# Results kept by channel: attention, gates and Fourier outputs of the first layer of a two-layer network

## The chip, the cores and the metric

One core of a Trainium2 chip. The metric is the time of one execution on the device, in microseconds (us); lower is better. The kernel before takes 3724.84 us, the median of three runs (3721.65 to 3726.13).

## The reference

A network of two layers over T = 2304 tokens (256 of context, 2048 latent) of width 1024. The change concerns the first layer alone:

```
h = layer_norm(x) * (1 + scale) + shift
q, ga, k, v, u, gb = split(h @ w_in)          # 768, 768, 256, 256, 256, 256
q, k = rope(rms_norm(q)), rope(rms_norm(k))   # 12 query heads of 64, 4 key heads
a = softmax(q k^T / 8) v                      # latent tokens see all 2304 keys, context tokens its own 256
f = real(fft2(rms_norm(u))) @ w_fmix
y = concat(a * silu(ga), f * silu(gb)) @ w_out
x = layer_norm(alpha * x + g * y) * gain + bias
```

The second layer (a bidirectional mLSTM) takes the result as its input. Everything is fp32, or products split into a high and a low part.

## The kernel before, in words

The program is written out for each engine: each has its own instruction order, and semaphores tie them. Tokens are handled in 18 tiles of 128. The stages run one after another: modulation, projections of layer 0 (names `pj_`, with the query heads `hq_` between them), key heads with the context's attention (`hd_`, `ca_`), attention of the latent tokens (`al_`), Fourier mix (`fo_`), the output of the mixer (`mo_`); then layer 1 (`pa_`, `pb_`, `ml_`, `mo_`).

**Projections** (`projections`). Steps k run over chunks c of 512 columns (five) and in each over the 18 tiles. A step multiplies a tile of `h`, split in `h_hi` and `h_lo` (stationary), with `whi` and `wlo` (512 columns moving): 8 slices of 128 channels, three products each (L245 to L247), into one of three PSUM banks. ScalarE (chunk 0 and, with SiLU, the gate chunks c = 3 and 4, L762) or VectorE copies the bank to `pj_stage` in the same step, and SyncE stores it to `s_proj`, token by token. Between these, every third step from k = 21 on, runs a tile of query heads: SyncE reloads the tile's queries and rope rows, ScalarE squares (L299), VectorE sums and turns, TensorE transposes (L370), ScalarE and VectorE take high and low part from PSUM (L306, L362), SyncE stores both to `s_q`.

**Context attention** (`ContextAttention`), twelve heads, its steps spread over the tiles of `heads`. The result stands token by token, with the sum of the weights in column 65; VectorE divides two columns (L1812) and multiplies 128x128 (L1814); POOL stores each head to `s_attn`.

**Attention** (`attention`). 48 blocks, each one query head with 512 tokens. TensorE computes all scores twice: first (`high_scores`, L2346) query by query in 20 products into three scratch banks `slots` (shown as `al_sx`), of which VectorE takes the maxima (L2269), and at the end of them the bias row `negm` (L2275). SyncE carries that row with four small DMAs (L2158) into the query operand `al_qb` of the block. The second time (`scores`, L2358/L2359), keys on the partitions, in nine pairs j of key tiles; ScalarE takes the exponential (L2209). The products with the values (L2368) go to the bank `acc`, even key tiles in partitions 0 to 63, odd ones in 64 to 127. POOL and VectorE add the nine pairs of exponentials (`al_asum`). The order in a body is the same on each engine: the body of block n holds the high scores of block n+1, the scores of n, and at its head the last values of n-1, which ScalarE copies to `al_ot` (L2216). Behind the scores of j = 7 TensorE runs `folded` for block n-1:

```
for i in range(nq):
    mm(fo[:, at:at + HD], ot[:, p % 2, cols], fold[:, 0:HD], start=True, stop=True)
    y = mm(fo[:, at + HD:at + HD + 1], asum[:, p % 2, cols], ones[:], start=True, stop=True)
```

It adds the two halves, turns the result to tokens and sums `asum` over partitions. `fo` is the third scratch bank. At j = 8 VectorE divides (L2290) and multiplies (L2294), and SyncE stores (L2164).

**Fourier** (`fourier`). 18 results of 128 tokens, token by token, copied by VectorE and stored to `s_four`; the loads of the out weights (`ow_wst`, two buffers) stand between the stores on SyncE, and ScalarE and POOL split them (L2452, L2456).

**Mixer's output** (`mixer_out`). Per tile: SyncE loads `attn`, `four` and the gate (`mo_in`), VectorE multiplies (`gated`, L2845), TensorE transposes 8 times (L2890), ScalarE takes the high part (L2759) and VectorE the low one (L2849), TensorE multiplies with the out weights (48 products of 512 columns), and VectorE and POOL add, norm and scale. `gated` runs two tiles ahead.

## Time and profile before

| | |
|---|---|
| runs (three) | 3724.84 us median, 3721.65 to 3726.13 |
| the profiled execution | 3726.69 us |
| its span on the core | 3724.9 us |
| TensorE | busy 3439.9 us (92%) |
| VectorE | 2280.6 us (61%) |
| ScalarE, GpSimd | 1336.0 us (36%), 1821.1 us (49%) |
| DMA | 480.18 MB, mean 129 GB/s |
| mean granted clock of TensorE | 0.959 of full speed |

PE is TensorE's products, PEld its weight loads, DVE VectorE, ACT ScalarE, POOL GpSimd, SP SyncE (SPq: its DMA issues). A row of a group says: line, engine, operation, what is written from what, shape, count, busy time and mean of one. "Idle before" is the time in which the engine did nothing ahead of it, with the instruction that ended it. The records of products overlap, since they are pipelined: the distance of two starts is what one costs.

### The profile page before, as it was taken

To read this page: it belongs to the slowest core of one execution; us is meant where nothing else is said; L and a number is where in the kernel's file an instruction comes from. 1 tells how busy PE (TensorE), PEld (TensorE's weight loads), DVE (VectorE), ACT (ScalarE), POOL (GpSimd) and SP (SyncE) were. 2 spreads that over 40 slices of the span, in tenths; PEclk is the share of its full clock that TensorE was granted. 3 is DMA by queue.
4 is the path that set the end of the run, shared out by engine and by line. 5 is a ranking of instruction groups with operands and counts; after the bars stand their busy time and mean duration, and the time that the engine had idled before them with its cause. 6 is when DMAs were issued, how large, how long until landed. Compare 5 with 4: busy or idle time off the path is not lost. (4 is left out here: it accounts for less than half of the span.)

```text
span 3724.9 us, 51223 instructions
## 1 busy us (share of the span) xinstructions
PE 3439.9 (92%) x16884; PEld 2590.2 (70%) x16884; DVE 2280.6 (61%) x3492; ACT 1336.0 (36%) x2240; POOL 1821.1 (49%) x1260
## 2 busy tenths in 40 slices
PE   6999997799999999999959979989999998999798
PEld 4787884456666666666548869878778786887587
DVE  4666642766666666666536664366575645777566
ACT  2432333434444444444420023333443422664300
POOL 1133323657777777777723333423586612444354
PEclk8999997799999999999979989999999999999899
DMA  5334535511111111111054445655545446677553
GB/s 189 99 107 132 142 105 177 191 27 35 34 35 34 34 35 36 36 38 35 17 198 166 166 166 171 203 186 158 180 129 172 140 151 197 215 220 243 201 210 146
DMA packets 357715, 480.18 MB, mean 129 GB/s; under 512 B 83308, under 2 KB 209276, under 8 KB 357392
## 3 DMA queue, kind: packets, MB, share of 16 engines
q1 hardware_dynamic: 296640, 360.01, 30.9%
q10 hardware_dynamic: 54256, 97.73, 8.8%
q0 software_dynamic: 6624, 19.94, 1.4%
q8 instruction: 109, 1.79, 0.2%
q14 instruction: 86, 0.70, 0.1%
HBM read 339.75 MB, written 137.72 MB: 128 GB/s over the span
## 5 line engine op out<-in xcount | busy, mean ns | idle before, releaser
L2269 DVE TENSOR_REDUCE al_mx<-al_sx 128x1 f32<-128x512 f32 (+1 forms) x960 | 562.6, 632 | 267.2 <-PE al_sx L2346 253.8
L2209 ACT ACTIVATE al_e<-al_st 128x1024 f32<-128x1024 f32 x432 | 443.1, 1027 | 579.4 <-PE al_st L2359 570.6
L2239 POOL TENSOR_TENSOR al_acc_p<-al_acc_p,al_e 128x1024 f32<-128x1024 f32 x192 | 457.4, 2382 | 19.8
L245 PE MATMUL pb_acc<-p_whi,pb_r_hi 128*128 128x512 f32 x952 | 378.5, 398 | 41.5 <-DVE pb_r_lo L1616 31.6
L2368 PE MATMUL al_acc<-al_e,vres 128*64 128x512 f32 x1728 | 402.5, 601 | 0.0
L247 PE MATMUL pb_acc<-p_whi,pb_r_lo 128*128 128x512 f32 x952 | 375.5, 394 | 0.0
L246 PE MATMUL pb_acc<-p_wlo,pb_r_hi 128*128 128x512 f32 x952 | 375.2, 394 | 0.0
L1616 DVE TENSOR_TENSOR pb_r_lo<-pb_stg,pb_r_hi 128x512 fp32r<-128x512 f32 x238 | 247.8, 1044 | 168.7 <-ACT pb_r_hi L1514 164.4
L2358 PE MATMUL al_st<-al_qa,kres 128*128 128x512 f32 x864 | 344.7, 399 | 3.7 <-DMA al_qb<-al_negm 3.2
L2359 PE MATMUL al_st<-al_qb,kres 128*128 128x512 f32 x864 | 340.3, 394 | 0.0
L2346 PE MATMUL al_sx<-kres,al_qx 128*128 128x512 f32 (+1 forms) x960 | 298.3, 393 | 13.4 <-DMA al_qx<-s_q 11.1
L2235 POOL TENSOR_TENSOR al_acc_p<-al_e 128x1024 f32<-128x1024 f32 x48 | 160.4, 3341 | 305.5 <-ACT al_e L2209 305.5
L245 PE MATMUL pj_acc<-pj_whi,pj_h_hi 128*128 128x512 f32 x720 | 286.8, 398 | 0.0
L2346 PEld LDWEIGHTS al_sx<-kres,al_qx 128*128 128x128 f32 x960 | 172.0, 191 | 162.3 <-issue 125.8
L246 PE MATMUL pj_acc<-pj_wlo,pj_h_hi 128*128 128x512 f32 x720 | 282.9, 393 | 0.0
L247 PE MATMUL pj_acc<-pj_whi,pj_h_lo 128*128 128x512 f32 x720 | 282.7, 393 | 0.0
L855 DVE TENSOR_TENSOR pj_h_lo<-pj_hall,pj_h_hi 128x1024 fp32r<-128x1024 f32 x90 | 135.1, 1502 | 210.3 <-ACT pj_h_hi L723 210.3
L2368 PEld LDWEIGHTS al_acc<-al_e,vres 128*64 128x64 f32 x1728 | 111.2, 136 | 211.2 <-issue 194.9
L1514 ACT ACTIVATE pb_r_hi<-pb_stg 128x512 fp32r<-128x512 f32 x238 | 149.4, 629 | 270.8 <-PE pb_acc L247 248.6
L245 PEld LDWEIGHTS pb_acc<-p_whi,pb_r_hi 128*128 128x128 f32 x952 | 181.3, 190 | 86.8 <-DVE pb_r_lo L1616 38.1
L245 PE MATMUL mo_acc<-ow_whi,mo_y_hi 128*128 128x512 f32 x544 | 215.6, 396 | 0.0
L246 PE MATMUL mo_acc<-ow_wlo,mo_y_hi 128*128 128x512 f32 x544 | 212.7, 391 | 0.0
(318 smaller groups left out, 7261.4 us busy)
## 6 DMA issues: line engine op xcount, KB each, us to landing
pb_stg<-s_hsum ACTq DMA_DIRECT2D x238, 256.0 KB, 2.8
s_proj<-pj_stage SPq DMA_DIRECT2D x90, 256.0 KB, 2.1
s_proj<-pb_out SPq DMA_DIRECT2D x72, 256.0 KB, 2.9
p_wst<-in_w1s ACTq DMA_DIRECT2D x18, 1024.0 KB, 6.5
ml_k<-s_proj SPq DMA_DIRECT2D x36, 512.0 KB, 4.3
ml_v<-s_proj SPq DMA_DIRECT2D x36, 512.0 KB, 8.7
mo_in<-s_proj SPq DMA_DIRECT2D x34, 512.0 KB, 5.7
hm_w<-in_ada_w SPq DMA_DIRECT2D x16, 1024.0 KB, 9.7
```

Of the source, the lines that this page charges most:

```text
L245: nc.tensor.matmul(out, s_hi, m_hi, start=start, stop=False)
L246: nc.tensor.matmul(out, s_hi, m_lo, start=False, stop=False)
L247: return nc.tensor.matmul(out, s_lo, m_hi, start=False, stop=stop)
L1616: V.tensor_tensor(r_lo[:, g % RING], stg[:, g % NSTG], r_hi[:, g % RING].bitcast(F32), ALU.subtract).then_inc(lo_done, 1)
L2209: nc.scalar.activation(e[:, pair(p, j), :, :], st[(NP * p + j) % 2][:, :, 0:W], ACT.Exp).then_inc(e_done, 1)
L2235: nc.gpsimd.tensor_tensor(acc_p[:], e[:, pair(p, 2)], e[:, pair(p, 5)], ALU.add).then_inc(add_p, 1)
L2239: nc.gpsimd.tensor_tensor(acc_p[:], acc_p[:], e[:, pair(p, j)], ALU.add).then_inc(add_p, 1)
L2269: V.tensor_reduce(mx[:, x:x + 1], slots[x % NSX][:, 0:spans[x % NS][1]], AX.X, ALU.max).then_inc(sx_max, 1)
L2346: mm(slots[x % NSX][:, 0:width], qx[:, p, i * P:(i + 1) * P], kres[:, g, lo:lo + width], start=True, stop=True).then_inc(sx_mm, 1)
L2358: mm(dst[:, t, 0:W], kres[:, g, keys], qa[:, p, :], start=True, stop=False)
L2359: y = mm(dst[:, t, 0:W], kres[:, NKV + g, keys], qb[:, p, :], start=False, stop=True)
L2368: y = mm(acc[t * HD:(t + 1) * HD, 0:W], vres[:, 2 * j + t, g, :], e[:, pair(p, j), t, :], start=(j == 0), stop=(j == NP - 1))
```

## The change

Five parts, all in layer 0.

1. *Projections.* In the gate chunks the weights become stationary and four tiles of tokens (512 columns) move, so gates leave by channel, into a new tensor `s_gt` (1024 x 2304). The products of four tiles are accumulated in four banks at once: the first two steps of such a quad run channels 0 to 511 for four column groups of the weights, the other two the rest. Five banks rotate in place of three, a step's eviction stands two steps later, `h_hi`/`h_lo` have four buffers. The last two tiles of a chunk form a pair (256 columns moving). The query heads' rows have two buffers in place of three, and share memory with the rotated products.
2. *Context attention* leaves by channel as well; one division (128x256) and two products (64x256) for two heads, a step later, and one store for two heads.
3. *Attention.* The fold is gone. VectorE adds the two halves itself (`joined`, L2376), behind the second maximum of a body, from PSUM and from ScalarE's copy of one half; the values of a block wait for it. Two blocks stand one above the other in `un` (ScalarE moves the even one: `keep_even`). TensorE sums `asum` of both blocks by two products of 512 columns (`denominators`, L2472) at j = 7 of every second body; VectorE divides 128x512 (L2381) at j = 8 there, and multiplies 128x512 (L2390) at j = 8 of the next body. Two DMAs store two blocks by channel.
4. *Fourier* writes by channel, and stays in SBUF (`four`); its stores are gone.
5. *Mixer's output.* No transposes. `attn` and the gates are loaded by channel (rows of 128 tokens, 512 bytes each), `gated` works in place and stands ahead of `norm`; high and low part read SBUF. The loads wait for the low part of the tile two ahead.

VectorE, attention, one body (names: `al_negm` the bias row, `al_rden` the divisors, `al_o` the result). Before, one body:

```order
L2269 TENSOR_REDUCE al_mx<-al_sx 128x1 x8
L2283 TENSOR_TENSOR al_acc_d<-al_e 128x1024
L2269 TENSOR_REDUCE al_mx<-al_sx 128x1 x8
L2286 TENSOR_TENSOR al_acc_d<-al_acc_d,al_e 128x1024
L2269 TENSOR_REDUCE al_mx<-al_sx 128x1 x4
L2275 TENSOR_REDUCE al_negm<-al_mx 128x4
L2290 RECIPROCAL al_rden<-al_sx 128x4
L2294 TENSOR_TENSOR al_o<-al_sx,al_rden 128x256
```

Now, from the end of an even body on:

```order
L2357 TENSOR_REDUCE al_negm<-al_mx 128x4
L2381 RECIPROCAL al_rden<-al_sx 128x512
L2351 TENSOR_REDUCE al_mx<-al_sx 128x1 x2
L2376 TENSOR_TENSOR al_even<-al_acc,al_ot 64x512
L2351 TENSOR_REDUCE al_mx<-al_sx 128x1 x6
L2365 TENSOR_TENSOR al_acc_d<-al_e 128x1024
L2351 TENSOR_REDUCE al_mx<-al_sx 128x1 x8
L2368 TENSOR_TENSOR al_acc_d<-al_acc_d,al_e 128x1024
L2351 TENSOR_REDUCE al_mx<-al_sx 128x1 x4
L2357 TENSOR_REDUCE al_negm<-al_mx 128x4
L2390 TENSOR_TENSOR al_o<-al_un,al_rden 128x512
```

The division stands once in two bodies, between the bias row and the next maxima, and the sum of the halves behind the second maximum of each body; the multiplication closes the other body.

TensorE, attention, scores of j = 7 and 8 (`al_st`) and the values behind them (`al_acc`). Before, in each body:

```order
L2359 MATMUL al_st<-al_qb,kres 128x512
L2380 MATMUL al_sx<-al_fold,al_ot 128x64
L2381 MATMUL al_sx<-al_ones,al_asum 128x1
L2380 MATMUL al_sx<-al_fold,al_ot 128x64
L2381 MATMUL al_sx<-al_ones,al_asum 128x1
L2380 MATMUL al_sx<-al_fold,al_ot 128x64
L2381 MATMUL al_sx<-al_ones,al_asum 128x1
L2380 MATMUL al_sx<-al_fold,al_ot 128x64
L2381 MATMUL al_sx<-al_ones,al_asum 128x1
L2358 MATMUL al_st<-al_qa,kres 128x512
```

Now, in every second body:

```order
L2453 MATMUL al_st<-al_qb,kres 128x512
L2468 ISA
L2470 REGISTER_ALU
L2472 MATMUL al_sx<-al_asum,al_ones 64x512 x2
L2448 REGISTER_ALU
L2452 MATMUL al_st<-al_qa,kres 128x512
```

Eight products (two instructions each in the trace) are gone from each body; two stand in every second one.

VectorE, mixer's output, one tile. Before:

```order
L2826 BN_AGGR mo_mv<-mo_stats 128x2
L2849 TENSOR_TENSOR mo_y_lo<-mo_tp,mo_y_hi 128x1024
L2831 TENSOR_SCALAR mo_r<-mo_r,mo_mv,mo_rstd 128x1024
L2835 TENSOR_TENSOR mo_fin<-mo_r,mo_gain 128x1024
L2845 TENSOR_TENSOR mo_y<-mo_in 128x1024
```

Now:

```order
L2911 BN_AGGR mo_mv<-mo_stats 128x2
L2942 TENSOR_TENSOR mo_y_lo<-mo_in,mo_y_hi 128x1024
L2927 TENSOR_TENSOR mo_in<-mo_in 128x768
L2929 TENSOR_TENSOR mo_in<-four,mo_in 128x256
L2916 TENSOR_SCALAR mo_r<-mo_r,mo_mv,mo_rstd 128x1024
L2920 TENSOR_TENSOR mo_fin<-mo_r,mo_gain 128x1024
```

The gating product is two, and ahead of the norm.

The core of the diff, in the order of the parts:

```diff
-    K, RING, NST, NACC, PIECES, NX = len(steps), 3 if L0 else 4, 3, 3, 2, 3
+    K, RING, NST, NACC, PIECES, NX = len(steps), 4, 3, 3, 2, 3
     by_act = [c == 0 or (L0 and c >= GATED) for c, _ in steps]
     KP = KD // PIECES
     mod = keep["mod"]
-    turned_q = [not L0 and C1_Q <= c * CH < C1_Q + D for c, _ in steps]
-    pair_of = [k - (t - CT) % 2 if turned_q[k] else k for k, (_, t) in enumerate(steps)]
-    last_use = [pair_of[k] + 1 if turned_q[k] else k for k in range(K)]
-    ahead = [min(K - 1, k + (1 if c == 0 else 2)) for k, (c, _) in enumerate(steps)]
+    turned_q = [c >= GATED if L0 else C1_Q <= c * CH < C1_Q + D for c, _ in steps]
+    base = [k - t % 4 if turned_q[k] else k for k, (_, t) in enumerate(steps)]
+    tiles = [min(4, NT - steps[base[k]][1]) if turned_q[k] else 1 for k in range(K)]
+    last_use = [base[k] + (k - base[k] if tiles[k] < 4 else 0 if k < base[k] + 2 else 3) if turned_q[k] else k for k in range(K)]
+    last_use = [base[k] + 1 if tiles[k] == 2 else last_use[k] for k in range(K)]
+    ahead = [min(K - 1, base[k] + (5 if tiles[k] == 4 and k > base[k] else 3) if turned_q[k] else k + (1 if c == 0 else 2)) for k, (c, _) in enumerate(steps)]
...
+    out_at = [k if not turned_q[k] else k + 1 if tiles[k] == 2 else k + 2 for k in range(K)]
+    outs = [[q for q in range(K) if out_at[q] == k] for k in range(K + 2)]
+    banks = acc + [tp[1][:, 0, :], tp[1][:, 1, :]]
+    T0 = turned_q.index(True)
+    bank_of = [k % NACC if k < T0 else (k - T0) % len(banks) for k in range(K)]
+    bank_before = [max((i for i in range(k) if bank_of[i] == bank_of[k]), default=None) for k in range(K)]
...
+                for q in outs[k]:
+                    out_of_psum(q)
...
+            def turned_products(k, c):
+
+                n, step, first = tiles[k], k - base[k], base[k]
+                if k == T0:
+                    pe.wait_ge(hf_dve, NT)
+                    pe.wait_ge(hf_act, NT)
+                if n == 4:
+                    pe.wait_ge(lo_done, first + (2 if step < 2 else 4))
+                    half, columns = step // 2, range(step % 2 * 2, step % 2 * 2 + 2)
+                    part = range(half * KP, half * KP + KP)
+                else:
+                    pe.wait_ge(lo_done, first + 2)
+                    half, columns, part = 1, range(2 * step, 2 * step + 2), range(KD)
+                for o in columns:
+                    at, user = o * P, first + o * n // 4
+                    if part[0] == 0 and (n == 4 or o % 2 == 0) and bank_before[user] is not None:
+                        evicted(pe, bank_before[user])
+                    dst = banks[bank_of[user]][:, o * n % 4 * P:(o * n % 4 + n) * P].rearrange("p (t n) -> p t n", n=P)
+                    for i in part:
+                        if first == first_of[c] and o == 0 and i % KP == 0:
+                            piece_low(pe, PIECES * c + i // KP)
+                        mm = split_mm(nc, dst, whi[:, c % 2, i, at:at + P], wlo[:, c % 2, i, at:at + P], moving(h_hi, k, i), moving(h_lo, k, i), i == 0, i == KD - 1)
+                    if half and (n == 4 or o % 2):
+                        mm.then_inc(mm_done, 1)
...
-        self.nc.vector.reciprocal(self.rden[:, n % 2, :], self.res[:, :, HD]).then_inc(self.rden_done, 1)
-        dve.wait_ge(self.rden_done, n + 1)
-        self.nc.vector.tensor_tensor(self.o[:, n], self.res[:, :, 0:HD], self.rden[:, n % 2, :].unsqueeze(2).broadcast_to([P, CT, HD]), ALU.mult).then_inc(self.o_done, 1)
+        self.nc.vector.reciprocal(self.rden[:], self.res[:, self.W:2 * self.W]).then_inc(self.rden_done, 1)
+        dve.wait_ge(self.rden_done, n // 2 + 1)
+        for i in range(2):
+            mine, other = slice(i * HD, i * HD + HD), slice((1 - i) * HD, (1 - i) * HD + HD)
+            self.nc.vector.tensor_tensor(self.o[mine, n // 2], self.res[mine, 0:self.W], self.rden[other], ALU.mult).then_inc(self.o_done, 1)
...
+                    act.wait_ge(un_done, n - 1)
+                half = slice(p * HD, (p + 1) * HD)
+                nc.scalar.activation(ot[half, :], acc[half, 0:W], ACT.Copy).then_inc(ot_done, 1)
+
+            def keep_even(v):
+
+                act.wait_ge(un_done, 2 * v + 1)
+                if not (fixed(v) and v == 0):
+                    act.wait_ge(o_done, v)
+                nc.scalar.activation(un[0:HD, :], even[:], ACT.Copy).then_inc(kept, 1)
...
+            def joined(n, p, v):
+
+                half, other = slice(p * HD, (p + 1) * HD), slice((1 - p) * HD, (2 - p) * HD)
+                dve.wait_ge(ot_done, n + 1)
+                if p == 0 and not (fixed(n) and n < 2):
+                    dve.wait_ge(kept, v)
+                V.tensor_tensor(even[:] if p == 0 else un[half, :], acc[other, 0:W], ot[half, :], ALU.add).then_inc(un_done, 1)
+
+            def inverse(v):
+
+                dve.wait_ge(den_mm, v + 1)
+                V.reciprocal(rden[:], fo[:, 0:W]).then_inc(rden_done, 1)
+
+            def norm(v):
+
+                dve.wait_ge(rden_done, v + 1)
+                dve.wait_ge(un_done, 2 * v + 2)
+                dve.wait_ge(kept, v + 1)
+                if not (fixed(v) and v == 0):
+                    dve.wait_ge(stored, v * 32)
+                V.tensor_tensor(o[:], un[:], rden[:], ALU.mult).then_inc(o_done, 1)
...
+                    if j == 0 and started:
+                        joined(n - 1, 1 - p, v if p else v - 1)
                     if j == 7 and nxt is not None:
                         bias(n + 1, 1 - p, v + p)
-                    if j == 8 and started:
-                        norm(n - 1, 1 - p, v - 1 + p)
+                    if j == 8 and p == 0 and started:
+                        inverse(v - 1)
+                    if j == 8 and paired:
+                        norm(v - 1)
...
-                    pe.wait_ge(ot_done, n)
+                    pe.wait_ge(un_done, n)
...
+            def denominators(n, v):
+
+                pe.wait_ge(asum_done, n + 2)
+                pe.wait_ge(sx_max, TOTAL * NX if fixed(n) and n + 2 >= TOTAL else n * NX + (3 * NX + 18))
+                if not (fixed(v) and v == 0):
+                    pe.wait_ge(rden_done, v)
+                for i in range(2):
+                    y = mm(fo[i * HD:(i + 1) * HD, 0:W], ones[:], asum[:, i, :], start=True, stop=True)
+                y.then_inc(den_mm, 1)
...
-                    if j == 7 and started:
-                        folded(n - 1, 1 - p)
-
-            pe.wait_ge(fold_ld, 16)
+                    if j == 7 and p == 0 and started:
...
+                tokens = four[:, :, 0:CTX] if j == 0 else four[:, :, CTX:T]
                 dve.wait_ge(o_mm, n + 1)
-                if n >= NO:
-                    dve.wait_ge(stored[n % NO], 16 * (n // NO))
-                V.tensor_copy(o[:, n % NO, :], po[n % 2][:, 0:FW]).then_inc(o_out, 1)
+                V.tensor_copy(tokens.rearrange("p h (m r) -> p h m r", r=R)[:, :, :, R - r if flip else r],
+                              po[n % 2][:, 0:FW].rearrange("p (h m) -> p h m", h=2)).then_inc(o_out, 1)
...
-                    sp.dma_start(ins[:, p, 0, 0:QW], s["attn"][rows, :]).then_inc(in_ld[p], 16)
-                    sp.dma_start(ins[:, p, 0, QW:D], s["four"][rows, :]).then_inc(in_ld[p], 16)
-                    sp.dma_start(ins[:, p, 1, :], s["proj0"][rows, C_GATE:W0_COLS]).then_inc(in_ld[p], 16)
+                    sp.dma_start(ins[:, p, 0, 0:QW].rearrange("p (k n) -> p k n", n=P), s["attn"][:, rows].rearrange("(k p) n -> p k n", p=P)).then_inc(in_ld[p], 16)
+                    sp.dma_start(ins[:, p, 1, :].rearrange("p (k n) -> p k n", n=P), s["gt"][:, rows].rearrange("(k p) n -> p k n", p=P)).then_inc(in_ld[p], 16)
...
+                if L0:
+                    dve.wait_ge(in_ld[p], 32 * v + 32)
+                    tokens = bass.ds(n * P, P)
+                    nc.vector.tensor_tensor(columns(p)[:, 0:KA, :], ins[:, p, 0, 0:QW].rearrange("p (k n) -> p k n", n=P),
+                                            ins[:, p, 1, 0:QW].rearrange("p (k n) -> p k n", n=P), ALU.mult)
+                    nc.vector.tensor_tensor(columns(p)[:, KA:KD, :], four[:, :, tokens],
+                                            ins[:, p, 1, QW:D].rearrange("p (k n) -> p k n", n=P), ALU.mult).then_inc(y_done[p], 1)
+                    return
...
                 tile(low_part, N, n, p, v, 1)
+                if L0:
+                    tile(gated, N, n, p, v, 2)
                 tile(norm, N, n, p, v, -1)
-                tile(gated, N, n, p, v, 2)
+                if not L0:
+                    tile(gated, N, n, p, v, 2)
```

## Rows read from the trace of the kernel before

**Rows 1.** Table by stretches: length; PE, PEld, DVE, ACT, POOL busy; clock; DMA share; GB/s
```profile
32.00:617.00 585.00, 533.61 (x2421) 439.76 (x2422) 327.66 (x397) 194.20 (x281) 150.69 (x104) 0.95 0.40 117
617.00:752.00 135.00, 96.09 (x447) 50.84 (x447) 85.46 (x221) 61.98 (x333) 91.65 (x122) 0.69 0.69 214
752.00:1866.00 1114.00, 1104.39 (x5162) 678.03 (x5162) 744.55 (x1177) 472.00 (x480) 793.47 (x336) 0.99 0.13 33
1866.00:1935.00 69.00, 37.27 (x296) 36.76 (x296) 29.01 (x65) 19.10 (x28) 18.16 (x8) 0.77 0.53 170
1935.00:2170.00 235.00, 215.92 (x1008) 179.71 (x1008) 149.66 (x183) 20.44 (x19) 69.43 (x60) 0.95 0.51 181
```

**Rows 2.** Timeline of TensorE in one attention block: start us, us, line, names
```profile
1208.39 0.33 PE L2380 MATMUL al_sx<-al_fold,al_ot 128*128 128x64 f32 x2
...
1210.10 0.49 PE L2358 MATMUL al_st<-al_qa,kres 128*128 128x512 f32 x1
1210.42 0.40 PE L2359 MATMUL al_st<-al_qb,kres 128*128 128x512 f32 x1
...
1211.21 2.80 PE L2368 MATMUL al_acc<-al_e,vres 128*64 128x512 f32 x12
1213.94 0.73 PE L2346 MATMUL al_sx<-kres,al_qx 128*128 128x512 f32 x2
```

**Rows 3.** Timeline of VectorE over the same microseconds
```profile
1208.71 0.17 DVE L2275 TENSOR_REDUCE al_negm<-al_mx 128x4 fp32r<-128x20 f32 x1
...
1214.48 3.66 DVE L2269 TENSOR_REDUCE al_mx<-al_sx 128x1 f32<-128x512 f32 x6 [3.47 <-PE al_sx L2346]
```

**Rows 4.** VectorE's divisions by tile: ns min/median/max, first and last start us
```profile
L1812 DVE RECIPROCAL ca_rden<-ca_res x12: 152/171/171, 663.8 to 724.7; 128x2 f32<-128x2 f32 x12
...
L1812 DVE RECIPROCAL ca_rden<-ca_res 128x2 f32<-128x2 f32 x12 | 2.0, 166 | 6.3 <-PE ca_res L1807 6.2
...
L2290 DVE RECIPROCAL al_rden<-al_sx x48: 182/183/184, 796.2 to 1865.6; 128x4 f32<-128x4 f32 x48
...
L3093 DVE RECIPROCAL ml_den<-ml_den x128: 162/164/166, 3151.8 to 3498.2; 128x1 f32<-128x1 f32 x128
```

**Rows 5.** A sum of 64x512 from PSUM in the key heads
```profile
L2020 DVE TENSOR_TENSOR kres<-hd_tk,kres x18: 673/677/683, 624.6 to 725.1; 64x512 fp32r<-64x512 f32 x18
```

**Rows 6.** The bias row's DMAs: the four issues in that block, all 192 (KB, us to landing)
```profile
1208.91 2.42 SPq L2158 DMA_DIRECT2D al_qb<-al_negm  x4
...
al_qb<-al_negm SPq DMA_DIRECT2D x192, 0.5 KB, 2.0
```

**Rows 7.** Timeline at attention's end
```profile
1862.03 0.66 PE L2380 MATMUL al_sx<-al_fold,al_ot 128*128 128x64 f32 x2 [7.24 <-issue]
...
1865.60 0.18 DVE L2290 RECIPROCAL al_rden<-al_sx 128x4 f32<-128x4 f32 x1 [13.90 <-PE al_sx L2381]
```

**Rows 8.** Products of 256 columns in a later stage, by tile
```profile
L246 PE MATMUL pa_acc<-pa_h_lo,p_whi x512: 278/283/420, 2191.3 to 2403.1; 128*128 128x256 f32 x171
```

**Rows 9.** Waits in the projections (us in total, times, longest)
```profile
ACT hq_hi L306 <- DMA s_q<-hq_lo: 148.0, 17, 14.2
...
PE pj_tp L370 <- DVE hq_lo L362: 7.5, 4, 3.5
```

**Rows 10.** Timeline of POOL at the end of the Fourier stage
```profile
1933.33 2.34 POOL L2456 TENSOR_TENSOR ow_wlo<-ow_wst,ow_whi 128x1024 fp32r<-128x1024 f32 x1 [1.84 <-ACT ow_whi L2452]
```

**Rows 11.** Timeline at the start of the mixer's output
```profile
1942.99 1.23 DVE L2845 TENSOR_TENSOR mo_y<-mo_in 128x1024 f32<-128x1024 f32 x1 [13.76 <-DMA mo_in<-s_proj]
...
1951.37 0.78 PE L245 MATMUL mo_acc<-ow_whi,mo_y_hi 128*128 128x512 f32 x1
```

**Rows 12.** Mixer's output, 1951 to 2163 us: the transposes as a group; VectorE's sum in one tile
```profile
L2890 PE MATMUL mo_tp<-keep_ident,mo_y 128*128 128x128 f32 x132 | 17.6, 277 | 0.0
...
2047.02 1.23 DVE L2816 TENSOR_TENSOR mo_r<-mo_acc,mo_gate 128x1024 f32<-128x1024 f32 x1 [3.67 <-PE mo_acc L247]
```

**Rows 13.** A load of 512 KB in rows of 512 bytes: KB, us to landing
```profile
ml_qt<-s_qt SPq DMA_DIRECT2D x32, 512.0 KB, 6.2
```

341 lines of the change are left out of this document (170 added, 171 removed).

## The prediction

> **What bounds the kernel now.** I read it in this order: a table by stretches (cut at the stages), TensorE's own timeline inside one attention block, then the same microseconds on VectorE and on SyncE's queue, and last the waits and first records of the stages around it. The table says that TensorE is the limit of three of the five stretches that the change touches: 533.61 of 585 us in the projections, 1104.39 of 1114 in attention, 215.92 of 235 in the mixer's output, at a granted clock of 0.95 to 0.99, so at the 2.4 GHz level nearly throughout [rows 1]. In the key heads with the context's attention (96.09 of 135 us, DMA share 0.69) and in the Fourier stage (37.27 of 69) it is not: loads and the last links of chains set their end. So an instruction taken off TensorE counts in full in attention and in the mixer's output, until another engine takes its place, and that one would be VectorE (744.55 us) [rows 1].
>
> **Attention, steady state.** The folding group (16 instructions, L2380/L2381) starts at 1208.39, and scores go on at 1210.10: 1.71 us, and the first pair of scores behind it stands 0.32 apart, 0.09 more than the 0.2275 of the products below, so 1.80 us per block [rows 2]. 48 blocks: -86.4 us. Instead, every second block has the denominators: two fp32 matmuls of 512 columns. A value product of this size is two records; 12 of them take 2.73 us (1211.21 to 1213.94), 0.2275 each [rows 2]. Four records are 0.91 us; with the change of operands at both ends, for which I take 0.2 (the groups around the fold lose 0.1 to 0.3), 1.1 us per pair, 24 pairs: +26.6. Net **-59.8 us**.
>
> What takes part of it back is on VectorE. Its maxima start 0.5 us behind the body's first product (1213.94, 1214.48) and run back to back, six in 3.66 us [rows 2, 3]. The new sum *joined* stands behind the second of them. It is a 64x512 sum from PSUM; the same form takes 0.677 us elsewhere [rows 5]. Since the scratch banks are three, the sixth product needs the third maximum, which now ends some 0.68 us later; about 0.35 us of slack lay there, and the copy `al_ot` in front of it is ready in time. I estimate 0.15 us of TensorE's wait per block: +7 us (ends 0 and 0.45 per block, 0 to +22, since the six maxima leave nearly no gap to catch up in).
>
> The division of 128x512 is the unknown. The trace has 128x1 at 164 ns, 128x2 at a median of 171 (mean 166) and 128x4 at 183 [rows 4]. From 2 to 4 elements that is 6.0 ns per element by the medians, 8.5 by the mean; on 183 ns, 508 more elements give 3.2 to 4.5 us. I take 7.3 ns, so 3.9 us. The denominators stand where the fold stood, and from its end at 1210.10 to the next body's first maximum at 1214.48 are 4.4 us [rows 2, 3]; less the end of the last product and the hand-over, 4.1, less the gap to the maximum, 3.9 to 4.0. So up to 3.9 us cost nothing; beyond it, maxima, scratch banks and TensorE slip one for one, 24 times: 0 at the low end, +13 at the high one. Being that near the edge, I put in +3. The multiplication of 128x512 in the odd body (some 0.7 us) replaces nothing there and lies in the same 4 us gap, free.
>
> Next late is the bias row. It is reduced at 1208.71, and four DMAs (issues over 2.42 us from 1208.91, 2.0 us each to landing) bring it to the block after, whose first scores are two products behind 1213.94, at about 1214.4 [rows 2, 3, 6]. The last issue starts near 1210.7 and lands near 1212.7: some 1.7 us of slack. Ahead of an even block the path is now 1.80 us shorter with no denominators in it, so the slack is about gone: some 0.1 us in 24 blocks and about 1 us in one or two that land late: 2.4 + 1.6, **+4** (0 to +10). ACT's `keep_even` (64x512, 0.6 us) and POOL's sums lie under 22 us of block: nothing. Attention's steady state: -59.8 + 7 + 3 + 4 = **-46**.
>
> **Attention's end.** The last fold begins at 1862.03 and the division at 1865.60: 3.57 us, at the lower clock level, since TensorE idled before [rows 7]. Now four long records (about 0.45 each, twice the 0.2275 at half the clock, 1.9 us) and 3.9 for the division stand against 3.57 + 0.18; with a product longer by 0.3 and a second DMA issue that is +2.5 (1.6 to 3.5).
>
> **Context attention.** A pair of heads had two divisions of 0.17 us [rows 4] and two products, and gets one division of 128x256 (1.7 to 2.3 us by the same slopes) and two products of half the rows and double the columns: some 1.7 us more per pair. While loads bound the stage (share 0.69 [rows 1]) that is hidden; the last of the twelve divisions, at 724.7 [rows 4], is in the tail, where a last pair and what it delays in VectorE's queue lie bare, twice. Six stores of 1 KB rows in place of twelve give some of it back. **+3** (0 to +5).
>
> **Projections.** The gate chunks keep their products: per tile 24 of 512 columns, whichever side is stationary. The two remaining tiles of each chunk run as 96 of 256 columns in place of 48 of 512; a record of the one kind lasts 0.283 us, of the other 0.40 [rows 8, 2], so 256 columns are 0.117 us and two halves cost what a whole does, to within 0.01, or 1 us for both chunks. The new cost is order: four tiles are accumulated at once, so the first bank is complete only after half the quad's 96 products of 0.2275 (10.9 of 21.8 us) and a quarter of the other half, 13.6 us, and ScalarE, whose program has this eviction ahead of the next head's copies, stands until then; behind it are SyncE's stores and VectorE. The heads' chain is already tight (ScalarE's `hq_hi` waits 148.0 us in all for the store of `hq_lo`; TensorE waits 7.5 us in 4 places for `hq_lo`) [rows 9]. I expect two stalls of 1 to 3 us where query tiles meet a quad's start: **+5** (0 to +15).
>
> **Fourier.** Eighteen stores go, and the copies write strided into SBUF. The stage's end was the last split of the out weights on POOL (1933.33 + 2.34), behind its load, not a store [rows 10]: **-1** (-2 to 0).
>
> **Mixer's output.** No transposes. The first product waited for gated (1942.99), transposes, ScalarE, VectorE and then a second gated and transposes: 1951.37 [rows 11]. Without both groups, and with high and low parts read from SBUF at 1.0 to 1.2 us each, it can start at about 1946.7: -4.7. From there 132 transposes are 17.6 us busy [rows 12]; 8 per tile are 1.07 us, less the 0.2 by which pipelined records overlap: 0.87, 16 tiles: -14. VectorE still idles 3.67 us per tile ahead of the sum [rows 12], so TensorE stays the limit. **-18.7** (-21 to -9). The loads are now 1,792 pieces of 512 bytes per tile; a 512 KB load of such rows takes 6.2 us to land [rows 13], and gate and attention together have about 48 products of 0.2275, 10.9 us, per tile: hidden, but not by much.
>
> **Sum:** -46 + 2.5 + 3 + 5 - 1 - 18.7 = -55.2. The profiled execution took 3726.7 us (span 3724.9), so 3671.5 by its count; it stands 1.9 above the median of the runs, 3724.84, so against that 3669.6: **3670**. With the ends named above this case's own range is 3648 to 3688. About 0.2% is what a measurement of this kernel can tell from no change.
>
> **Rivals.**
> - *Quads hold the projections' chain* (0.13). If the three engines behind a quad's first eviction lose 5 to 8 us in each of three or four quads that still carry query tiles, the stage is 25 longer: about 3690. For it: 148 us of waiting in that chain [rows 9]; against it: TensorE waited only 7.5 us for it.
> - *The mixer becomes DMA-bound* (0.07). If the short pieces need over 11 us per tile, 16 us of the gain go: 3686. Against: 6.2 us for half a megabyte of them [rows 13].
> - *Nothing new is waited for* (0.12): joined, row and heads cost nothing, and the projections' existing 7.5 us of waits go as the steps are rearranged: 3648.
> - *The division binds attention* (0.05), the other side. The fastest 128x2 record is 152 ns [rows 4]; from there to 183 it is 15.5 ns per element, 8.1 us for 512. The point from which it decides is a division of 6.3 us (12 ns per element): 2.4 us beyond the free 3.9, 24 times, eat the other 55. At 8.1 us attention gets 101 us of waits: some 3765. Against it: 171 and 183 are far more frequent, and one element costs 164.
> - *The division costs every element the same, at the upper slope* (0.2). By the means, 8.5 ns [rows 4]: 4.5 us, 0.55 past the free 3.9, 24 times: +13 in place of +3, and +0.6 each at attention's end and in the context's last pairs: 3682. For it is the mean, against it the medians' 6.0. The Trainium skill, "VectorE: DVE Perf Modes", section "First, the fixed hardware budget", has Reciprocal as an iterative divide on the first two slices with a repeat count of 8, and gives VectorE 0.96 GHz; as an estimate from that page, 8.3 ns per element and 4.4 us, which would make the time 3679. The rows allow it and don't show it.
>
> **Chances.** Forecast 0.43; the rivals 0.13 (quads), 0.07 (DMA), 0.12 (no new wait), 0.05 (division binds) and 0.2 (upper slope). Everything but the division that binds, and a hundredth of the quads, is faster by over 0.2%: faster 0.93; same 0.02, where a division of 6 us would land; slower 0.05. The range 3645 to 3696 leaves out the far half of *nothing new*, the division that binds, and the far third of the quads: 0.06 + 0.05 + 0.04, and little of the others.
>
> **What would show it.** Right: the attention stretch 1065 to 1078 us long instead of 1114 [rows 1]; no L2380 fold and 96 denominators' records of 0.23; the division at 3.2 to 4.5 us in its own row; TensorE's waits for VectorE in attention under 15 us; the mixer's first product near the fourth microsecond after gated and no `mo_tp`. Wrong: a division over 5 us; waits of TensorE on the bias row over 10 us; `hq_lo` or `pj_stage` as releaser of over 15 us of TensorE's idle time in the projections; `mo_in` as a releaser in the mixer.

## The result: slower by 0.6%, where 1.5% faster was forecast

The changed kernel takes 3742.15 us (median of 8 runs, 3735.33 to 3749.57), the one before in the same series 3720.36 us (8 runs, 3710.40 to 3726.49). The ratio is 1.0057, with a 95% interval of 1.0046 to 1.0069. The forecast was 3670, with a range of 3645 to 3696 and a chance of 0.05 for slower; so the time lies outside the range and on the other side.

The profiled execution has a span of 3740.1 us, 15.2 more than before. I cut both traces at the same events: the end of TensorE's last product of the projections, the start of its first of attention, the start of the last division of attention, the end of the last product of the Fourier stage, the start of the first of layer 1. Lengths in us:

| stretch | before | after | change | forecast |
|---|---|---|---|---|
| projections, to their last product | 603.2 | 615.2 | +12.0 | +5 |
| key heads with context attention | 132.6 | 152.5 | +19.9 | +3 |
| attention, to its last division | 1129.8 | 1130.5 | +0.7 | -46 |
| attention's end and Fourier | 63.2 | 68.4 | +5.2 | +1.5 |
| mixer's output | 251.6 | 231.3 | -20.3 | -18.7 |
| all behind | 1544.5 | 1542.2 | -2.3 | 0 |

The table of stretches of the kernel after, cut there (columns as in [rows 1]):

```profile
32.00:615.20 583.20, 538.24 (x2516) 446.44 (x2516) 315.97 (x385) 188.65 (x262) 142.50 (x101) 0.96 0.38 112
615.20:767.70 152.50, 95.36 (x425) 43.22 (x425) 89.37 (x203) 65.28 (x352) 88.93 (x119) 0.68 0.64 205
767.70:1898.20 1130.50, 1084.54 (x4512) 595.05 (x4512) 853.01 (x1198) 483.49 (x504) 812.75 (x336) 0.99 0.13 33
1898.20:1966.60 68.40, 37.86 (x296) 37.46 (x296) 35.15 (x65) 17.92 (x27) 14.78 (x7) 0.75 0.40 132
1966.60:2197.90 231.30, 198.99 (x865) 164.13 (x864) 156.84 (x208) 22.08 (x20) 85.33 (x64) 0.94 0.54 178
```

Attention of the kernel before, in the same cut:

```profile
735.80:1865.60 1129.80, 1116.58 (x5184) 684.32 (x5184) 756.79 (x1198) 472.00 (x480) 793.47 (x336) 0.99 0.13 33
```

In attention TensorE has less to do, and it now waits: 46 us idle of 1130.5, where it was 13 of 1129.8. VectorE went from 757 to 853 us of work. The gain was made and given back in the same stage, to the microsecond. TensorE's waits from 770 to 1860 us of the kernel after, which leaves out the stage's first 2 and last 38 us (us in total, times, longest):

```profile
PE al_sx L2440 <- DVE al_mx L2351: 31.0, 55, 1.6
PE al_st L2452 <- DMA al_qb<-al_negm: 3.2, 1, 3.2
PE al_st L2452 <- issue: 1.2, 1, 1.2
```

The bias row, which I had feared, is waited for once. What TensorE waits for are VectorE's maxima. VectorE's own list of the same 1090 us says why they are late:

```profile
DVE al_mx L2351 <- PE al_sx L2440: 184.4, 203, 4.9
DVE al_acc_d L2365 <- POOL al_acc_p L2324: 33.9, 31, 1.9
DVE al_rden L2381 <- PE al_sx L2472: 16.8, 22, 0.8
```

The second line is what is new: 31 times VectorE waits for POOL. Before, it did so twice, at the first and at the last block. Here is one of them on VectorE's timeline (start us, us), in a body that begins at 1245.45 with TensorE's first high score:

```profile
1245.99 1.29 DVE L2351 TENSOR_REDUCE al_mx<-al_sx 128x1 f32<-128x512 f32 x2 [2.69 <-PE al_sx L2440]
1247.31 0.68 DVE L2376 TENSOR_TENSOR al_un<-al_acc,al_ot 64x512 f32<-64x512 f32 x1
1248.03 2.22 DVE L2351 TENSOR_REDUCE al_mx<-al_sx 128x1 f32<-128x512 f32 x4
...
1253.03 2.35 DVE L2365 TENSOR_TENSOR al_acc_d<-al_e 128x1024 f32<-128x1024 f32 x1 [1.28 <-POOL al_acc_p L2324]
1255.29 2.21 DVE L2351 TENSOR_REDUCE al_mx<-al_sx 128x1 f32<-128x512 f32 x4
...
1265.81 3.36 DVE L2381 RECIPROCAL al_rden<-al_sx 128x512 f32<-128x512 f32 x1 [0.73 <-PE al_sx L2472]
1270.10 1.29 DVE L2351 TENSOR_REDUCE al_mx<-al_sx 128x1 f32<-128x512 f32 x2 [0.93 <-PE al_sx L2440]
...
1275.79 1.23 DVE L2365 TENSOR_TENSOR al_acc_d<-al_e 128x1024 f32<-128x1024 f32 x1
```

The same on POOL and on TensorE:

```profile
1240.37 10.12 POOL L2321 TENSOR_TENSOR al_acc_p<-al_acc_p,al_e 128x1024 f32<-128x1024 f32 x4
1250.57 2.36 POOL L2324 TENSOR_TENSOR al_acc_p<-al_acc_p,al_acc_d 128x1024 f32<-128x1024 f32 x1
1253.01 1.29 POOL L2328 TENSOR_TENSOR al_asum<-al_acc_p 128x512 f32<-128x512 f32 x1
...
1275.84 2.31 POOL L2328 TENSOR_TENSOR al_asum<-al_acc_p 128x512 f32<-128x512 f32 x1 [0.16 <-POOL al_acc_p L2324]
```

```profile
1254.68 0.39 PE L2440 MATMUL al_sx<-kres,al_qx 128*128 128x512 f32 x1
1256.03 0.50 PE L2440 MATMUL al_sx<-kres,al_qx 128*128 128x512 f32 x1 [0.96 <-DVE al_mx L2351]
```

The reader is to see a chain. VectorE's first sum of a block (L2365) overwrites `al_acc_d`; POOL adds `al_acc_d` of the block before into its own sum as the last of six additions, and that ends at 1252.93. VectorE starts 0.1 us later, its next maxima follow the sum, and TensorE, whose three scratch banks are full, stands 1.12 us longer than the 0.23 between two products. In the kernel before the same pair stood like this:

```profile
1217.11 2.39 POOL L2242 TENSOR_TENSOR al_acc_p<-al_acc_p,al_acc_d 128x1024 f32<-128x1024 f32 x1
...
1219.71 2.23 DVE L2283 TENSOR_TENSOR al_acc_d<-al_e 128x1024 f32<-128x1024 f32 x1
```

POOL was through at 1219.50, VectorE came at 1219.71: 0.2 us of slack. Count from a body's first high score (1213.94 here). POOL's chain of sums starts 12.9 us behind it and takes 15.7 us up to the read of `al_acc_d`, so it ends 28.5 us after its body began. With bodies of 22.97 us that is 5.6 us into the next, and VectorE wants the buffer at 5.8. With a body that is 1.6 us shorter the chain would end at 7.2. In the kernel after it ends at 7.5 (1252.93 against 1245.45), behind a body of 21.84. VectorE, itself later by the new sum, is there at 6.3 and waits 1.28 us. Its sum of exponentials then lasts 2.35 us beside POOL's next one, in place of 1.23 as in the body behind.

Most periods of the bodies in the kernel after are 24.11 and 21.84 us in turn. The long one holds the denominators, which cost 1.02, and the wait, which stands in the body behind a short one. Their sum, 45.95, is what two bodies took before, 45.94.

### The profile page after: what moved, and what is told of

Its sections match the earlier page's. It is cut to its first block and busy times, and to the rows that moved or that the text cites. A ratio compares the mean times of both kernels' runs of the same rounds, so it can differ in the third digit from the quotient of the medians.

```text
span 3740.1 us, 49669 instructions
## 1 busy us (share of the span) xinstructions
PE 3408.4 (91%) x16164; PEld 2493.0 (67%) x16164; DVE 2392.2 (64%) x3504; ACT 1344.6 (36%) x2264; POOL 1838.3 (49%) x1254
## 5 line engine op out<-in xcount | busy, mean ns | idle before, releaser
L2440 PE MATMUL al_sx<-kres,al_qx 128*128 128x512 f32 (+1 forms) x960 | 317.6, 402 | 45.6 <-DVE al_mx L2351 31.0
L899 DVE TENSOR_TENSOR pj_h_lo<-pj_hall,pj_h_hi 128x1024 fp32r<-128x1024 f32 x90 | 122.6, 1378 | 213.4 <-ACT pj_h_hi L759 213.4
L247 PE MATMUL mo_acc<-ow_whi,mo_y_lo 128*128 128x512 f32 x544 | 213.3, 392 | 0.0
L2452 PEld LDWEIGHTS al_st<-al_qa,kres 128*128 128x128 f32 x864 | 162.9, 189 | 71.8 <-issue 31.0
L247 PEld LDWEIGHTS pb_acc<-p_whi,pb_r_lo 128*128 128x128 f32 x952 | 181.7, 191 | 40.6
```

The source lines that it names most:

```text
L247: return nc.tensor.matmul(out, s_lo, m_hi, start=False, stop=stop)
L2440: mm(slots[x % NSX][:, 0:width], qx[:, p, i * P:(i + 1) * P], kres[:, g, lo:lo + width], start=True, stop=True).then_inc(sx_mm, 1)
L2452: mm(dst[:, t, 0:W], kres[:, g, keys], qa[:, p, :], start=True, stop=False)
```

## The experiments

Theories: **A** POOL's read of `al_acc_d`. **B** the sum of the halves on VectorE. **C** the long division. For the context's stretch: **D** the division stands in VectorE's queue ahead of the keys' rotation, TensorE idles and its clock falls; **E** the products with the values; **F** the divisions' own time alone. Each run is told by the stretches as cut above.

### e1_sum_early

```diff
                 for i, j in enumerate(IN_POOL[2:]):
                     pool.wait_ge(e_done, n * NP + j + 1)
                     pool.wait_ge(add_p, n * 5 + i + 1)
+                    if i == 1:
+                        pool.wait_ge(add_d, n * 2 + 2)
+                        nc.gpsimd.tensor_tensor(acc_p[:], acc_p[:], acc_d[:], ALU.add).then_inc(comb_done, 1)
+                        pool.wait_ge(comb_done, n + 1)
                     nc.gpsimd.tensor_tensor(acc_p[:], acc_p[:], e[:, pair(p, j)], ALU.add).then_inc(add_p, 1)
-                pool.wait_ge(add_d, n * 2 + 2)
                 pool.wait_ge(add_p, n * 5 + 5)
-                nc.gpsimd.tensor_tensor(acc_p[:], acc_p[:], acc_d[:], ALU.add).then_inc(comb_done, 1)
-                pool.wait_ge(comb_done, n + 1)
```

> Edit: POOL adds VectorE's partial sum al_acc_d as its third addition, not as its last, so that the buffer is free some 7 us earlier; the same work. Theory A (VectorE's first sum of a block waits for POOL to have read al_acc_d of the block before, which its 16 us chain of sums ends 7.0 us into a body that follows a short block; VectorE's maxima stand behind that sum, and TensorE's high scores behind them): the wait of 1.28 us and TensorE's gap of 1.12 us go, in every second block, with a part of the 0.5 us by which the two engines slow each other; attention from 1130 to 1095 to 1105 us, the kernel to 3706 to 3716. Theory B (the sum of the halves ahead of the third maximum is what costs): attention stays at 1130 within 4 us. Theory C (the division of 3.36 us holds the maxima): unchanged as well.

Measured: 3706.4 us against 3718.86 of the kernel before, ratio 0.9965 (0.9953 to 0.9977). Attention is 1098.0 us, bodies 22.92 and 21.83. TensorE's waits there (of its list, the first two lines):

```profile
PE al_sx L2441 <- DVE al_mx L2352: 6.4, 32, 0.7
PE al_st L2453 <- DMA al_qb<-al_negm: 3.3, 1, 3.3
```

No wait of VectorE for POOL is left in its list. Same additions, another order: 32.5 us, against the kernel after. Theory A stands. B and C fall as the cause of this loss; what the sum of the halves costs besides is the matter of e5, e9 and e10. This order of six additions alone turns the change from a loss into a gain.

### e2_no_halves

The sum of the halves is left out, so this kernel does not compute attention:

```diff
-                V.tensor_tensor(even[:] if p == 0 else un[half, :], acc[other, 0:W], ot[half, :], ALU.add).then_inc(un_done, 1)
+                V.memset(mark[:], 0.0).then_inc(un_done, 1)
...
-                    pe.wait_ge(un_done, n)
+                    pe.wait_ge(ot_done, n)
```

> Left out: the sum of the two halves of the attention result (a 1-column memset stands for it), so latent attention is not computed; the values of the next block wait for ScalarE's copy instead. Theory A: only the two short gaps at the sixth high score go, 0.3 us per block at most, and where the wait for POOL ends last nothing: attention 1130 to between 1116 and 1126 us. Theory B: the sum is the cause, attention falls by 35 us or more, below 1095. Theory C: unchanged, 1130.

Measured: 3724.59 us in one run; attention 1125.7 us, as A has it. The short bodies fall to 21.37, the long ones stay at 24.12: whatever time the sum gives back, VectorE waits for POOL instead (51.7 us in 44 places, 33.9 in 31 with the sum). While POOL held the long body, the sum of the halves cost little: 4.8 us in all of attention.

### e3_ctx_short_division and e4_ctx_division_behind

The first divides 2 of 256 columns in the context's `norm`, so the context's attention is not divided as it should be. The second moves the division, with the two multiplications behind it, and leaves nothing out:

```diff
             for n in range(NT):
-                blocks(dve, n, (ca.norm, 7))
                 if n:
                     products(n)
                     turned(n)
                 scaled(n)
-                blocks(dve, n, (ca.bias, 3))
+                blocks(dve, n, (ca.norm, 7), (ca.bias, 3))
```

> Left out: the division of the context's attention is done for 2 columns of 256, six times 0.17 instead of 1.76 us; the rest is constant. From TensorE's last product of the projections to the first of attention were 132.6 us before and 152.5 after the change. Theory D (the division stands in VectorE's queue ahead of the key heads' rotation, TensorE idles for it, its granted clock falls to the 1.2 GHz level, and all its products of the stage take twice as long): that stretch falls by 12 to 18 us, and the clock of the stretch comes back over 0.8. Theory E (the products with the values, twice the time per head since 256 columns move twice, set the pace): by 3 us at most. Theory F (only the 9.5 us of six divisions themselves count): by 8 to 10 us at an unchanged clock.

> Edit: in the heads' loop on VectorE the context's division and products stand behind the rotation of the keys, which TensorE's transposes wait for, and not ahead of it; nothing is left out. Theory D: TensorE gets its transposes 2.6 us earlier in every second step, but then waits at the values for the bank that the division reads; 4 to 12 us of the 20 come back, with the clock of the stretch somewhat higher. Theory E: nothing changes (within 2 us). Theory F: nothing, the divisions are as long as before.

Measured, in one run each: 3721.26 and 3728.51 us. The stretch from the last product of the projections to attention:

```profile
615.20:749.20 134.00, 83.19 (x425) 37.83 (x425) 80.05 (x204) 65.06 (x352) 91.49 (x119) 0.74 0.74 233
```

```profile
619.20:755.70 136.50, 85.74 (x426) 38.11 (x425) 90.17 (x203) 65.04 (x352) 89.90 (x119) 0.73 0.73 229
```

Against 152.5 that is -18.5 and -16.0. But this stretch is not the same from run to run: the kernels in which it is untouched had 152.5 (after), 149.4 (e1), 141.8 (e2), 149.3 (e5), 148.5 (e6) and 148.5 (e10). Against their mean of 148.3 the two gain 14 and 12 us. The two later kernels with the edit of e4 had 137.2 (e7) and 135.1 (e9), so the gain is not one run's luck. Theory E falls: the products with the values are the same in all. F falls by e4, which has every division at its full 1.76 us (90.17 us of VectorE against 89.37) and is as fast within 2.5 us as the one without them: where it stands, the length costs; behind the rotation it does not. Of D the queue is shown. TensorE's waits for the rotation (`hd_rot`), in the kernel after and in e4:

```profile
PE hd_tk L2128 <- DVE hd_rot L2080: 43.7, 11, 14.3
```

```profile
PE hd_tk L2127 <- DVE hd_rot L2080: 31.9, 11, 14.2
```

The clock is shown only in part. In the loop (680 to 720 us) the kernel after had these rows, e3 the ones behind them:

```profile
680.00:700.00 20.00, 16.65 (x74) 8.17 (x70) 12.60 (x25) 9.53 (x57) 10.91 (x20) 0.59 0.71 236
700.00:720.00 20.00, 16.17 (x68) 7.84 (x64) 13.01 (x27) 7.88 (x41) 10.22 (x14) 0.64 0.56 172
```

```profile
680.00:700.00 20.00, 15.96 (x113) 8.01 (x112) 17.62 (x45) 14.10 (x78) 17.41 (x25) 1.00 1.03 340
700.00:720.00 20.00, 17.66 (x94) 10.19 (x93) 12.98 (x34) 10.81 (x59) 14.58 (x21) 0.74 0.68 216
```

At a granted clock of 0.59, mostly the 1.2 GHz level, TensorE is busy 16.65 of 20 us with 74 instructions; at 1.00, the 2.4 GHz level, 15.96 with 113. So the gaps that the queue opened seem to cost also by the lower level behind them. Over the whole stretch, however, the clock rose only from 0.68 to 0.74, not over 0.8 as I had expected, and e2 with 0.76 still took 141.8. The kernel before the change had the stretch in 132.6 us at 0.71, and with e8's edit in 134.0 at 0.67, so the mean clock doesn't set its length. How much of the 14 us is clock and how much is queue stays open.

### e5_halves_later

```diff
-                    if j == 0 and started:
+                    if j == 2 and started:
                         joined(n - 1, 1 - p, v if p else v - 1)
```

(with the edit of e1)

> Edit: the early partial sum of the run before, and the sum of the halves moved on VectorE from behind the second maximum of a body to behind the sixth, where VectorE had 0.36 us of idle time before TensorE's next high scores; the same work. Theory B2 (with POOL's wait gone, what is left above the nominal body is the sum of the halves in the stretch in which VectorE has no slack: 0.46 us in the short bodies of 21.83, which are 21.38 without it, and as much in the long ones of 22.91): attention from 1098 to between 1074 and 1082 us, bodies of 21.4 and 22.4. Rival G (the bias row's DMAs, now that bodies are short, end last): 1090 or more, with TensorE waiting on al_qb. Rival H (values wait for the sum instead): 1088 to 1098, with waits of the values' products on al_un or al_even.

Measured: 3707.33 us, ratio 0.9958 (0.9945 to 0.9972); attention 1096.2, bodies 22.87 and 21.78. Rival H it is, a miss of mine. TensorE's waits:

```profile
PE al_acc L2463 <- DVE al_even L2377: 7.3, 23, 0.3
PE al_acc L2463 <- DVE al_un L2377: 7.0, 23, 0.3
```

The maxima's wait is gone (0.7 us are left of it) and the values' products wait in its place, 0.3 us in each body. The sum has a window of one maximum's length, not an open end.

### e6_tiles_ahead

```diff
-    ahead = [min(K - 1, base[k] + (5 if tiles[k] == 4 and k > base[k] else 3) if turned_q[k] else k + (1 if c == 0 else 2)) for k, (c, _) in enumerate(steps)]
+    ahead = [min(K - 1, base[k] + (5 if tiles[k] == 4 and k > base[k] + 1 else 3) if turned_q[k] else k + (1 if c == 0 else 2)) for k, (c, _) in enumerate(steps)]
+    for k in range(K):
+        if turned_q[k] and not turned_q[k - 1]:
+            ahead[k - 2] = k + 1
```

> Edit to the change's projections alone: the second tile of the first quad is prepared two steps ahead and not one, and ScalarE and VectorE prepare the next quad's first two tiles one step later, so that in between the query heads are not held up; the same work. After the change TensorE stood 4.13 us before the first quad, then 3.13, 0.94, 1.68 and 0.63 us, with 3.2 us more in products at the lower clock behind these. Theory J (these stops are ScalarE held behind the query heads' store and behind the quad's first bank): the first stop goes and the others halve; the last product of the projections ends at 606 to 610 us in place of 615. Rival K (quads cost it in TensorE's own time, by narrow products and changes of the stationary side): 613 to 617.

Measured: 3729.82 us in one run, last product of the projections at 606.4 in place of 615.2; the five stops have become one of 2.39 us, and the products at the lower clock behind them are gone. Theory J stands. The projections' end itself differs from run to run: without this edit it was at 615.0 to 619.2 in seven kernels, with it at 606.4, 606.4 (e7) and 604.0 (e9). In the kernel after, the first stop read like this on ScalarE and VectorE:

```profile
400.12 0.81 ACT L310 ACTIVATE hq_hi<-pj_tp 128x768 fp32r<-128x768 f32 x1 [13.02 <-DMA s_q<-hq_lo]
400.82 1.05 ACT L759 ACTIVATE pj_h_hi<-pj_hall 128x1024 fp32r<-128x1024 f32 x1
```

```profile
401.90 1.23 DVE L899 TENSOR_TENSOR pj_h_lo<-pj_hall,pj_h_hi 128x1024 fp32r<-128x1024 f32 x1 [6.45 <-ACT pj_h_hi L759]
```

A quad's first step needs two tiles where a step needed one, the second was to be prepared a step later, and there ScalarE stood behind the store of the query heads until 400.12. TensorE resumed at 403.34.

### e7_all_four

> All four edits together: early partial sum, later sum of the halves, context's division behind the keys' rotation, tiles ahead. If they add up: attention 1076, key heads with context attention 136 to 142 in place of 152, projections' end 608; 3740 - 54 - 13 - 6 gives 3662 to 3675, a ratio of 0.984 to 0.989 to the kernel before. If shortening one stage lengthens another, over 3680.

Edits of e4, e5 and e6 (with e1's). Measured: 3681.21 us (3676.00 to 3682.57), ratio 0.9889 (0.9873 to 0.9906). Stretches: 606.4, 137.2, 1096.3. They add up to within 4 us: from e1's 3706.4, 8.8 us of the projections and 12.2 of context attention (149.4 to 137.2) leave 3685.4; e5's part gives nothing in attention, as when it stood alone with e1's.

### e8_before_sum_early

The edit of e1, on the kernel before.

> Edit to the kernel before: POOL adds VectorE's partial sum as its third addition, not its last. Theory A says that this buffer came free just in time there (0.2 us ahead of VectorE's next first sum), so nothing is waited for: attention stays at 1130 within 3 us. If the buffer had been a limit before as well, it would fall by 10 us or more.

Measured: 3729.46 us in one run (the kernel before in its series: 3721.68, 3715.25 to 3728.90); attention 1127.0 us in place of 1129.8, every body but a few at 22.97, where before they were at 22.97 to 23.05. One of the first is 23.32 in place of 24.81: there VectorE waited 1.84 us for POOL. So at the stage's start the buffer cost 1.5 us in the kernel before, and behind it nothing, or 0.08 us a body at most. The wait in every second body was made by shortening the body. The run as a whole is no faster, since its projections ended 4.7 us later.

### e9_halves_fifth

```diff
-                    some(AHEAD[j])
-                    if j == 0 and started:
-                        joined(n - 1, 1 - p, v if p else v - 1)
+                    some(1 if j == 2 else AHEAD[j])
+                    if j == 2:
+                        if started:
+                            joined(n - 1, 1 - p, v if p else v - 1)
+                        some(AHEAD[j] - 1)
```

(with the edits of e1, e4 and e6)

> Edit: the four edits of the run before, but the sum of the halves stands behind the fifth maximum of a body, not behind the sixth. Behind the sixth it ended 0.3 us too late for the values' first product (14.3 us of TensorE's waits in 46 bodies). A maximum of 512 columns takes 0.6, so behind the fifth the sum ends 0.3 us ahead of the values, and the sixth maximum, which no product needs before the values are through, is late by the sum's 0.68 without cost. Theory: the waits on al_even and al_un go, bodies of 21.4 and 22.5, attention from 1096 to 1078 to 1084 us, kernel 3660 to 3672, ratio 0.984 to 0.987. Rival: the first sum of exponentials and the high scores behind it slip instead (TensorE waits on al_mx 0.2 us or more per body), attention 1090 or more. Rival G: the bias row's DMAs end last at bodies of 21.4: TensorE waits on al_qb in over ten bodies.

Measured: 3670.66 us (3666.86 to 3671.68), ratio 0.9861 (0.9843 to 0.9880). Attention 1085.6, bodies 21.38 and 22.76. The stretches, up to the Fourier stage's end:

```profile
32.00:604.00 572.00, 532.55 (x2508) 442.57 (x2508) 320.35 (x383) 189.40 (x263) 144.97 (x101) 0.96 0.39 115
604.00:739.10 135.10, 85.13 (x425) 38.34 (x425) 90.33 (x203) 65.05 (x352) 90.28 (x119) 0.76 0.73 231
739.10:1824.70 1085.60, 1068.69 (x4512) 595.06 (x4512) 842.29 (x1199) 483.69 (x504) 840.48 (x336) 0.99 0.14 35
1824.70:1892.40 67.70, 37.68 (x296) 37.20 (x296) 35.08 (x65) 17.92 (x27) 14.47 (x7) 0.73 0.40 133
```

The waits on `al_even` and `al_un` are gone, those on the bias row are one of 3.3 us. My theory had the mechanism; the size is off by 2 us. The short bodies are the 22.97 of before less 1.60 for the fold; the long ones keep 0.37 us beyond that and the denominators.

### e10_sum_early_no_halves

> Left out: the sum of the halves of the attention result, so latent attention is not computed; POOL's early partial sum is in. What the sum costs at all once POOL is out of the way, and what attention can reach: by the short bodies without it (21.38) and the denominators' 1.02, pairs of 43.8 us, attention 1074 to 1078. If it stays at 1090 or more, something else holds bodies at 21.8, and the sum was not the cost.

Left out as in e2, with POOL's early sum. Measured: 3694.4 us in one run, attention 1086.8, bodies 21.37 and 22.76. It is no faster than e9, which computes everything: behind the fifth maximum the sum of the halves is free. The 0.37 us of the long body stand here too: 0.1 at its start, the rest around its twelfth high score. Ahead of that VectorE's first sum of exponentials is long. In e9, in a short and in a long body:

```profile
1182.50 1.21 DVE L2368 TENSOR_TENSOR al_acc_d<-al_e 128x1024 f32<-128x1024 f32 x1
```

```profile
1204.10 2.16 DVE L2368 TENSOR_TENSOR al_acc_d<-al_e 128x1024 f32<-128x1024 f32 x1
```

In the long one POOL's last addition runs beside it: that ends 7.5 us into the body, behind a short one at 6.2. So POOL's chain reaches into the next body here as well, in a milder form. No run takes this away, so it is read from the trace and not shown.

## Why the prediction was wrong

**The bound.** "TensorE is the limit ... until another engine takes its place, and that one would be VectorE" was right in name and not carried through. I looked at VectorE's busy time and at its maxima, and did not ask what its sums wait for.

**The step that failed** is half a sentence: "POOL's sums lie under 22 us of block: nothing". I compared POOL's work with the length of a block, which is a question of throughput, and POOL has about 5 us of idle time in each block even now (4.7 or 5.7, ahead of its first sum). The chain's end counts: VectorE's next block writes what POOL reads last. 0.2 us of slack stood against 1.6 us that the change takes from a body. It cost 32.5 us (after against e1). Attention is 46.7 us short of its forecast in all, and the terms account for it to within 1 us: 32.5 here, 7.5 for the fold, 5.4 for the sum of the halves beyond its 7, about 9 for the 0.37 us in 24 long bodies, less the 7 that I had put in for the division and the bias row and that did not come.

**The fold's removal** was over-counted. I took 1.80 us per body. TensorE's timeline of the kernel after, around the place where the fold was, in a body without denominators:

```profile
1241.28 0.40 PE L2453 MATMUL al_st<-al_qb,kres 128*128 128x512 f32 x1
1241.60 0.50 PE L2452 MATMUL al_st<-al_qa,kres 128*128 128x512 f32 x1
1241.93 0.40 PE L2453 MATMUL al_st<-al_qb,kres 128*128 128x512 f32 x1
```

From the last score of j = 7 to the second of j = 8 are 0.65 us; with the fold between them they were 2.26 (one product of 0.23 ahead of 1208.39, to 1210.42 [rows 2]). So 1.60 is gone, which is also what lies between the bodies of before and the short ones of e9 (22.97 and 21.37): the long first pair, which I had put down to the fold, belongs to the scores. The denominators cost 1.02 (forecast 1.1; 24 of them are 26.4 and not the 26.6 of the sum). 48 x 1.60 - 24 x 1.02 = 52.3 in place of 59.8.

**The sum of the halves**, forecast at 0.15 us per body with 0.45 as the upper end, cost 0.45 in short bodies (21.83 with it, 21.37 without) and 0.15 in long ones (22.92 and 22.76): from e1 to e9 attention falls by 12.4 us. The term was 7: right in mechanism, near the upper bound half the time. That it could be had free by its place I had not looked for.

**The division**, by VectorE's records of it in the kernel after:

```profile
L2381 DVE RECIPROCAL al_rden<-al_sx x24: 3357/3358/3358, 850.8 to 1898.2; 128x512 f32<-128x512 f32 x24
```

```profile
L1881 DVE RECIPROCAL ca_rden<-ca_res x6: 1739/1758/1758, 680.4 to 755.1; 128x256 f32<-128x256 f32 x6
```

It takes 3357 to 3358 ns, each of 24 times. On the 183 ns of four columns that is 6.25 ns per element, near the 6.0 of the medians [rows 4]; I took 7.3 and 3.9 us. VectorE has 0.93 us of idle time behind it, so it is free, as forecast, and neither rival about it came. The context's 128x256 takes 1.76 us. The estimate of 8.3 ns per element and 4.4 us that I had worked out from the Trainium skill's page "VectorE: DVE Perf Modes" (section "First, the fixed hardware budget"; the clock stands in its "Specifications") does not hold here: these records show a quarter less per element.

**The bias row**, +4, cost nothing: one wait of 3.2 us in all of attention, and the kernel before has one of 3.2 us as well.

**Attention's end**: from the start of the last sums over partitions to the first product of the Fourier stage were 17.0 us (1862.03 to 1879.07) and are 19.9 (1896.18 to 1916.11): +2.9 against +2.5. In the table it is spread over two rows, since the cut lies at the division: 1.5 us less ahead of it, 4.4 more from it on, of which 3.36 - 0.18 is the division itself.

**Context attention**, +3, was +19.9 in this pair of profiles, and +15.7 by the mean of the six kernels in which the stretch is as the change left it; 12 to 14 us of that go when the division is moved or cut short. I called the stage bound by loads until its tail and put the divisions under them. Its loads are themselves paced by this loop: the DMA share fell from 0.75 to 0.64, and is 0.73 in e4. VectorE, TensorE and the loads wait for each other in turn there, so that 2.1 us more on VectorE in every second step are in the chain, though VectorE is busy only 89 of 152 us. This is the second step that failed: "While loads bound the stage (share 0.69 [rows 1]) that is hidden".

**Projections**, +5, were +12, in profiles whose end differs by 4 us from run to run (603.2 and 607.9 before the change, 615.0 to 619.2 with it). The stalls behind quads' starts came (3.13, 0.94 and 1.68 us), and one of 4.13 us ahead of the first quad that was not in my list. The rival *Quads hold the projections' chain* had the mechanism, with a size of 25.

**Fourier**, -1: the span of its products went from 49.7 to 50.5, so nothing.

**Mixer's output**, -18.7: -20.3. The first product stands 3.7 us behind `gated` instead of 8.4:

```profile
1977.68 0.96 DVE L2927 TENSOR_TENSOR mo_in<-mo_in 128x768 f32<-128x768 f32 x1 [10.44 <-DMA mo_in<-s_gt]
...
1981.38 0.79 PE L245 MATMUL mo_acc<-ow_whi,mo_y_hi 128*128 128x512 f32 x1 [14.76 <-DVE mo_y_lo L2942]
```

and its loads in pieces of 512 bytes land in 4.8 us (median), fast enough. This was the part whose every wait I had followed. The total is closer than its parts, though, and that is luck: 4.7 us of it lie between `gated` and the first product, as forecast, 12.5 behind that product, where 14 were forecast, and 3.1 ahead of `gated`, which starts 11.1 us behind the last Fourier product in place of 14.2 and stands in no term.

**The chances.** 0.05 for slower was laid on one mechanism, the division. The error is to have put the rest of the risk into terms of known kind, each with its own small bound, and none into a shared buffer that nobody in the sum had looked at. Of the signs that were to show it wrong in attention and in the projections none came: the division takes 3.36 us, TensorE waits 3.2 for the bias row and 11.1 for `hq_lo` and `pj_stage`. The one that pointed at the cause stood among those for right: TensorE's waits for VectorE in attention, 31.0 us and not under 15. That e9 takes 3670.66 us where 3670 was forecast is chance: it has four edits more, and its terms are others.
